# Two projection tiles in seven half-size block products, sums of weights on GpSimd, and rotary rows by transfers, in a two-layer hybrid decoder step

## What is computed

```python
h = rmsnorm(x, norm_g)
proj = h @ w_in                      # 1024 -> all columns below
qkv_a, z_a, beta, alpha, f_b, z_b, qkv_c, z_c, gate_raw = split(proj)
o_a = rmsnorm(gated_delta(silu(conv(qkv_a)), ...)) * silu(z_a)      # mixer a
o_b = rwkv7(token_shift_mix(f_b), ...)             * silu(z_b)      # mixer b
q_c = rope_partial(rmsnorm(q_c, qn_c), pos)                          # mixer c
k_c = rope_partial(rmsnorm(k_c, kn_c), pos)
o_c = attention(q_c, past_k + k_c, past_v + v_c)   * silu(z_c)
up    = [o_n @ w_branch[n] for n in (a, b, c)]       # 512 -> 1024
gates = sigmoid(gate_raw + b_gate)                   # 3 x 1024
x = x + sum(gates * up) @ w_out
x = x + sigmoid(x @ w_pg + b_pg) * (p @ w_ple)
```

## Time and profile before

| | us |
|---|---|
| median of 3 runs (1301.18 to 1306.65) | 1301.43 |
| profiled execution | 1299.52 |
| its span, first to last instruction | 1297.6 |
| PE busy, share | 1254.5, 97% |
| DVE busy, share | 594.6, 46% |
| ACT busy, share | 369.1, 28% |
| POOL busy, share | 136.8, 11% |
| mean granted TensorE clock | 0.993 |

### The profile page before, as it was taken

One profiled execution on the slowest core, in us unless ns is written; L12 is line 12 of the kernel. 1 busy time (PEld: TensorE's weight loads), 2 busy tenths in 40 slices (PEclk: granted clock), 3 DMA queues, 4 the chain that ended last, 5 costly groups with the idle time before them and its releaser, 6 DMA issues. The chain is left out here.

```text
span 1297.6 us, 23527 instructions
## 1 busy us (share of the span) xinstructions
PE 1254.5 (97%) x9334; PEld 954.2 (74%) x9334; DVE 594.6 (46%) x1269; ACT 369.1 (28%) x802; POOL 136.8 (11%) x204
## 2 busy tenths in 40 slices
PE   8999999999999999999999999999999999999998
PEld 6768866787687676767767787677866866767776
DVE  3655466644545523331254645475446454251212
ACT  2342212422233343310124322134124223433001
POOL 0112023020120110000001120210101101100000
PEclk9999999999999999999989999899999999999999
DMA  6832135412302565354245312543123035652631
GB/s 215 232 103 67 27 109 182 126 35 66 84 19 88 145 197 178 115 179 146 67 147 151 109 55 58 156 134 97 34 68 98 18 114 158 199 161 74 212 97 36
DMA packets 142215, 147.75 MB, mean 114 GB/s; under 512 B 15096, under 2 KB 129822, under 8 KB 141980
## 3 DMA queue, kind: packets, MB, share of 16 engines
q1 hardware_dynamic: 138492, 136.37, 34.5%
q0 software_dynamic: 3616, 9.89, 2.7%
HBM read 135.17 MB, written 11.07 MB: 113 GB/s over the span
## 5 line engine op out<-in xcount | busy, mean ns | idle before, releaser
L1073 PE MATMUL psum<-x_a,ring 128*128 128x288 f32 x1296 | 343.8, 416 | 2.3 <-ACT shift_in L1647 1.2
L1073 PE MATMUL psum<-x_b,ring 128*128 128x288 f32 x1296 | 338.5, 411 | 2.9 <-ACT shift_in L1647 1.2
L1073 PEld LDWEIGHTS psum<-x_a,ring 128*128 128x128 f32 x1296 | 242.2, 193 | 75.2 <-issue 13.8
L1073 PEld LDWEIGHTS psum<-x_b,ring 128*128 128x128 f32 x1296 | 239.0, 190 | 74.1 <-issue 15.0
L1647 ACT ACTIVATE arena<-psum 128x512 f32<-128x512 f32 (+9 forms) x206 | 96.8, 488 | 196.4 <-PE psum L1000 79.3
L1073 PE MATMUL psum<-z,ring 128*128 128x288 f32 x384 | 102.3, 413 | 1.2 <-issue 1.2
L1073 PEld LDWEIGHTS psum<-z,ring 128*128 128x128 f32 x384 | 70.1, 190 | 22.0 <-issue 4.8
L1000 PE MATMUL psum<-consts,arena 128*128 128x128 f32 (+2 forms) x446 | 64.2, 278 | 8.5 <-DMA arena<-in_x_prompt 5.5
L1000 PEld LDWEIGHTS psum<-consts,arena 128*128 128x128 f32 (+2 forms) x446 | 51.0, 144 | 27.3 <-issue 10.3
L1073 PE MATMUL psum<-merged,ring 128*128 128x288 f32 x256 | 62.6, 407 | 2.2 <-DVE merged L2099 2.2
L1647 ACT ACTIVATE arena<-arena 128x256 f32<-128x256 f32 (+7 forms) x104 | 44.8, 464 | 66.5 <-DVE arena L2577 27.9
(11 more groups left out here) (341 smaller groups left out, 1601.6 us busy)
## 6 DMA issues: line engine op xcount, KB each, us to landing
ring<-in_w_in SPq DMA_DIRECT2D x72, 1024.0 KB, 5.3
ring<-in_w_branch SPq DMA_DIRECT2D x24, 512.0 KB, 3.6
arena<-in_cache_k SPq DMA_DIRECT2D x32, 256.0 KB, 3.0
arena<-in_cache_v SPq DMA_DIRECT2D x32, 256.0 KB, 3.0
ring<-in_w_out SPq DMA_DIRECT2D x8, 1024.0 KB, 7.0
ring<-in_w_pg SPq DMA_DIRECT2D x8, 1024.0 KB, 4.9
arena<-in_state_dn SPq DMA_DIRECT2D x8, 512.0 KB, 8.3
out_dn_sample<-arena POOLq DMA_DIRECT2D x8, 512.0 KB, 4.7
```

What stands on the lines that cost most here:

```text
L1073: ins = mm(out[:, 0:NTOK], lhs, rhs(k), **flags)
```

## The change

**Pairs.** `p_z`, `p_c` and `p_g` are made two tiles at a time (`pair`, 24 pairs a layer). The 1024 x 256 block of weights and the 1024 x 288 block of h are each cut into 2 x 2 quarters: weights of 4 K-steps by 128 channels, h of 4 K-steps by 144 tokens. The 2 x 2 product is made in seven products of quarters instead of eight (the Winograd form). A pair is 14 "parts" of 2 K-steps, 4 instructions each, 56 instructions of 144 columns instead of 32 of 288, in two of the three banks. It needs

- four sums of h quarters per layer (`w_t`, VectorE, 128 x 576 each), written over X(l), which goes to DRAM (`x_kept`) in `a_conv(l,0)` and comes back in `p_g 23`, on SP's queue;
- four sums of weight quarters per pair (GpSimd, 128 x 512 each, 192 in all), after the parts 4, 8 and 12 of the pair before (`sums_at`); PE waits for them on `w_s` at parts 2, 4, 6 and 10;
- putting the products together: ScalarE copies one product (144 columns) after part 1 and two (288 columns) after part 5, VectorE does five additions of 144 columns after part 9, one after part 11 and one at the end. PE waits for ScalarE's copies (`w_kept`) at parts 6 and 10 and for VectorE's first two additions (`w_u`) at part 12. Before, ScalarE alone read these banks, and no later matmul of the same tile waited for that.

**Ring** of 3 places instead of 4. **Gates** leave PSUM without scale and bias; `g_tanh` is one operation of 288 columns per gate (8, 8, 6 and 2 of them) with scale and bias in it. **Rotary:** the permutation matmuls are gone. In `c_rms`, SP issues 6 transfers per tensor that move the rows to partner partitions (12 a layer), and 6 tiny ones turn the gains. VectorE does its three 1152-column operations in `c_rms`, ahead of the norm factor, and one in `c_rope`. **Order:** `FILL` is new, fillers are counted in parts, both `c_rms` stand together ahead of the cache fetches. Several semaphores are shared by steps that used one each.

```diff
-RING = 4
+RING = 3
+WIDE = ("p_z", "p_c", "p_g")
+PARTS = 14
...
+            def pair(l, part):
...
+                w, x, out = ((a11, b11, one[:, 0]), (WS[:, 0], t[:, 0], two[:, 0]), (a21, t[:, 2], two[:, 1]),
+                             (WS[:, 1], t[:, 1], one[:, 1]), (a12, b21, one[:, 2]), (WS[:, 2], b22, two[:, 2]),
+                             (a22, t[:, 3], one[:, 0]))[q]
...
+                elif part == 6:
+                    pe.wait_ge(S.sem("w_s"), 4 * no + 3)
+                    pe.wait_ge(S.sem("w_kept"), 2 * no + 1)
...
+                elif part == 12:
+                    pe.wait_ge(S.sem("w_u"), S.count("w_u"))
+                for k in (2 * (part % 2), 2 * (part % 2) + 1):
+                    ins = mm(out, w[:, k, :], x[:, k, :], start=k == 0, stop=k == 3, skip_group_check=True)
...
+                if m[-1] == 10:
+                    dve.wait_ge(S.sem("w_kept"), S.count("w_kept"))
+                    room_for(dve, order[final])
+                    tt(WP[:, 3, :], WP[:, 0, :], one[:, 1], ADD)
+                    tt(out[0], WP[:, 0, :], one[:, 2], ADD).then_inc(S.sem("w_u"), 1)
+                    dve.wait_ge(S.sem("w_u"), S.count("w_u"))
+                    link(tt(WP[:, 1, :], WP[:, 1, :], WP[:, 3, :], ADD))
+                    tt(out[3], WP[:, 1, :], WP[:, 2, :], ADD)
+                    link(tt(WP[:, 2, :], WP[:, 2, :], WP[:, 3, :], ADD))
...
+                    ins = (lambda: tt(WS[:, 0], a21, a22, ADD), lambda: tt(a21, a11, a21, SUB),
+                           lambda: tt(WS[:, 1], WS[:, 0], a11, SUB), lambda: tt(WS[:, 2], a12, WS[:, 1], SUB))[q]()
+                    ins.then_inc(S.sem("w_s"), 1)
...
-            def c_rope(l, i):
-                pe.wait_ge(S.sem("inv_roots"), S.count("inv_roots"))
-                pe.wait_ge(S.sem("c_rope"), S.count("c_rope", S.at - 1))
-                pe.wait_ge(S.sem("c_n"), S.count("c_n"))
-                for h in range(4):
-                    ins = mm(M[h][:, 0:NTOK], C("swap"), QC[:, 4 * i + h, :], start=True, stop=True)
-                ins.then_inc(S.sem("c_sw"), 1)
...
+                for to, of, n in turned:
+                    sp.dma_start(CSW[to:to + n, i, :, :], QC[of:of + n, 4 * i:4 * i + 4, :]).then_inc(S.sem(f"c_sw{i}"), 16)
...
-                fn(gates(n, part), gates(n, part), ACT.Tanh).then_inc(S.sem("g_tanh"), 1)
-                act.wait_ge(S.sem("g_tanh"), S.count("g_tanh"))
+                first, last = ((0, 7), (8, 15), (16, 21), (22, 23))[n + part]
+                evicted(act, "p_g", l, last)
+                for m in range(first, last + 1):
+                    ins = fn(gate(m), gate(m), ACT.Tanh, scale=0.5, bias=Phalf("b_gate", m))
```

More of the change, by code:

```diff
@@ L265 @@
     "c_qx": {"c_nat": (1, lambda st: st[2] == 0)},
+    "w_p": {"lead": (1, lambda st: st[2] in WIDE and st[-1] % 2 == 0)},
+    "w_kept": {"lead": (1, lambda st: st[2] in WIDE and st[-1] in (2, 6))},
+    "w_u": {"w_t": (1, None), "lead": (1, lambda st: st[2] in WIDE and st[-1] == 10)},
+    "x_moved": {"a_conv": (16, lambda st: st[2] == 0), "p_g": (16, lambda st: st[2] == 23)},
     "merged": {"p_up": (1, lambda st: st[2] > 0)},
@@ L268, with banks_of, sums_at @@
 }
+wide_lead = lambda st, part: st[0] == "lead" and st[2] in WIDE and st[-1] == part
 PROJECTIONS = ("p_a", "p_z", "p_ba", "p_f", "p_c", "p_g", "p_up", "p_y", "p_pg", "p_ple")
+def banks_of(st):
+    return 0 if st[0] not in PROJECTIONS else 2 if st[0] in WIDE else 1
+def sums_at(order):
+    ends = [i for i, st in enumerate(order) if banks_of(st)]
+    at, no = {}, 0
+    for before, last, i in zip([-1] + ends, ends, ends[1:]):
+        if order[i][0] not in WIDE:
+            continue
+        if order[last][0] in WIDE:
+            for part, qs in ((4, (0, 1)), (8, (2,)), (12, (3,))):
+                j = [j for j in range(before + 1, last) if wide_lead(order[j], part)]
+                at[j[0]] = [(no, q) for q in qs]
+        else:
+            j = [j for j in range(before + 1, last) if order[j][0] == "lead"]
+            at[j[0]] = [(no, q) for q in range(4)]
+        no += 1
+    return at
 class Steps:
@@ L279, in __init__ @@
             self.tally(name, [self.by(st, where) for st in order])
-        projections = [int(st[0] in PROJECTIONS) for st in order]
-        number = np.cumsum(projections) - 1
+        takes = [banks_of(st) for st in order]
+        first = np.cumsum(takes) - takes
         for b in range(3):
-            self.tally(f"bank{b}_read", [int(p and n % 3 == b) for p, n in zip(projections, number)])
+            self.tally(f"bank{b}_read", [sum((n + i) % 3 == b for i in range(k)) for k, n in zip(takes, first)])
+        sums = sums_at(order)
+        self.tally("w_s", [len(sums.get(i, ())) for i in range(len(order))])
     @staticmethod
@@ L480, in whole, with pair, branch_z @@
         out.append(s)
+    def pair(*s):
+        for a in range(PARTS - 1):
+            out.append(("lead",) + s + (a, a + 1))
+        out.append(s)
+    def branch_z(n):
+        for half in range(2):
+            pair("p_z", n, 2 * half + 1)
+            out.append(("z_silu", n, half))
     for m in range(NA):
@@ L2012, in y_out @@
                 fn(STG[96:128, 2, m // 4, :], y_banks(m)[2][96:128], ACT.Copy).then_inc(S.sem("y_rows_a"), 1)
-            do = dict(params_load=params_load, x_in=x_in, p_ple=p_ple, y_out=y_out, params=params, norm=norm, p_a=p_a, p_f=p_f, p_c=p_c, p_z=p_z, z_silu=z_silu, p_g=p_g, g_tanh=g_tanh, p_pg=p_pg, p_ba=p_ba,
+            do = dict(params_load=params_load, x_in=x_in, p_ple=p_ple, y_out=y_out, params=params, norm=norm, p_a=p_a, p_f=p_f, lead=lead, z_silu=z_silu, g_tanh=g_tanh, p_pg=p_pg, p_ba=p_ba,
                       a_convout=a_convout, a_silu=a_silu, a_sq=a_sq, a_beta=a_beta, a_l2=a_l2, a_rows=a_rows, a_scale=a_scale, a_pairs=a_pairs,
```

337 lines of the change are left out of this document (214 added, 123 removed), and 16 rows, old and new, of the table FILL.

## The result

The changed kernel takes **1456.23 us** (median of 4 runs, 1446.71 to 1459.3) against 1301.66 before on the same chip: 1.1165 times as long, 95% interval 1.1107 to 1.1224. I had forecast slower, 1317, with a range up to 1340. The direction was right; of 155 us I had foreseen 15. Some executions fall in a slower state of the chip, with a lower clock (here one of e9), and the ratios with an interval leave those out.

The account below looks back on a forecast made before the run. PE's nearly full matmul stream (97% busy) was taken as the bound. Per layer −25.2 (stream) + 12.5 + 16.0 (waits) + 4.4 (port) = +7.7, so +15.4 on 1299.5, 1314.9; as a median 1317 us, range 1283 to 1340.

Parts of the forecast that it names:

- The stream: PE's matmuls: 144-column instructions take 123 ns each; with the permutation matmuls gone, 25.2 us a layer saved, 50.4 in all.
- The order waits: PE waiting for ScalarE and VectorE, which work in order: 12.5 plus 16.0 us a layer lost.
- the 7.1 worked out: At b_lora(0,0), behind b_mix on VectorE: PE waits 7.1 us instead of 1.8.
- 5.14 for 4.1: At part 12 of p_c 5: PE waits 4.1 us for VectorE additions standing behind b_kk.
- 3.9 for 2.9: At the second c_rms, now right behind the first: PE waits 2.6 + 0.3 us for Ln and Exp.
- The term of 7.9 us a layer: Five pairs, p_c 9 to p_g 5, beside mixer b's chunk chain: three quarters of 10.5 us of VectorE additions delay PE.
- The 16.0 us a layer of that paragraph: Rest of the layer: waits of 7.9 beside the chunk chain, 3.3 at c_rms, 2.8 at gates, about 2.0 at softmax.
- The port: GpSimd's sums slow VectorE's SBUF operations: 2.9 us in b_mix and 1.5 in b_kk, 4.4 a layer (0 to 9.6).
- a bound of 9.6 us a layer: Port cost in b_mix and b_kk if each 4.8 us of GpSimd sums blocks VectorE whole, instead of 4.4.
- rival D: Clock falls behind PE's long waits add 7 to 14 us; with the port's cost whole, up to 1340; chance 0.25.
- Transfers: The 12 row transfers a layer on SP, ahead of the cache fetches: hidden by the stream of p_g, no cost.
- my sum without it gave 1308: Rival case: the sums of waits hold but the port costs nothing, 1317 − 9 = 1308; chance 0.15.

Follow-up runs that it names:

- e9: Changed kernel with GpSimd's sums cut to 8 columns for the 12 p_c pairs only, a quarter of all pairs: 1.0888 of before (1.074 to 1.1036).
- e1: Changed kernel with the same 192 GpSimd sums in the same places and with the same waits, but 8 columns each instead of 512: 1345.33 us.
- e11: Kernel of e1 with VectorE's seven additions per pair cut to 8 columns as well, waits kept: 1346.8 us.
- e12: Changed kernel with each pair's three VectorE additions of two SBUF inputs replaced by scaled copies of one input: 1437.23 us.
- e13: Kernel before with five GpSimd fills of 128 x 512 behind each of 96 tiles, reading nothing: 1308.07 us against 1300.63.
- e3: Kernel before with 192 GpSimd sums of 128 x 512 added, two behind each of 96 tiles, results unused: 1371.28 us.
- e5: Changed kernel with useless matmuls ahead of PE's waits, 80 at b_lora(l,0) and 30 at the second c_rms: 1456.61 us.
- e6: Kernel of e1 with useless matmuls ahead of PE's waits, 62 at b_lora(l,0) and 30 at the second c_rms: 1349.22 us.
- e15: Kernel before with the same six holds as e14, but PE does 62 useless matmuls in each: 1369.52 us.
- e10: Kernel before with the rotary part alone: row transfers and VectorE's new order in place of the permutation matmuls: 1295.81 us against 1300.06.
- e8: Changed kernel with 7 of the 12 parts ahead of both c_rms moved between them, in both layers: 1467.51 us.
- e14: Kernel before with PE held idle six times at p_f 1, 3 and 5 of both layers, until GpSimd finishes 20 fills: 1367.91 us.

## Why the prediction was right in sign and wrong in size

| | before | e1 | changed |
|---|---|---|---|
| time, us | 1301.66 | 1345.33 | 1456.23 |
| span | 1297.6 | 1342.7 | 1453.6 |
| PE busy | 1254.5 | 1237.7 | 1280.5 |
| span less PE busy | 43.1 | 105.0 | 173.1 |
| VectorE busy | 594.6 | 692.1 | 803.6 |
| mean granted clock | 0.993 | 0.969 | 0.939 |

**The stream.** In undisturbed stretches eight 144-column instructions start 0.98 us apart (216.07 to 217.05 in e1), 122.5 ns each. I had taken 123. Right.

```profile
216.07 1.14 PE L1208 MATMUL psum<-x_a,weight_sums 128*128 128x144 f32 x8
217.05 1.14 PE L1208 MATMUL psum<-x_a,ring 128*128 128x144 f32 x8
```

**The order waits.** I had summed 28.5 us a layer, 57 in all. e1, where GpSimd is out of the way, has 105.0 − 43.1 = 62 us more of idle PE. `b_lora` waits 7.08 us for the 7.1 worked out (up to 9.6 in the changed kernel). At `p_c 5` it is 5.14 for 4.1, at part 10 behind ScalarE and not at part 12 behind VectorE: the producer that is late (`b_kk`) is the same, the engine through which it reaches PE another. The second `c_rms` waits 3.9 for 2.9. The term of 7.9 us a layer, for additions of 2.1 us a pair in VectorE's queue, has no support: with 1.2 us a pair (e11) nothing changes. The 16.0 us a layer of that paragraph were otherwise not tested one by one. So that the sum of 57 lies near 62 is in part luck.

**The port: the step that failed.** I had read the stretching from the earlier trace rows, and priced it in two stretches a layer only, `b_mix` and `b_kk`: 4.4 us a layer, at most 9.6. It costs 111 us, 55 a layer, over ten times as much. Three things were missing in that step. First, the sums stand beside the whole middle of each layer: of the 819 VectorE operations without a PSUM input, 149 took over 0.1 us more than the shortest of their line and form, against 56 in e1. Second, an operation of 0.3 us can wait for a whole GpSimd operation of 1.3 us, so it loses by the number of meetings, not by its own length. The 93 further ones lost 112 us together, 1.2 us each, and a sum lasts 1.27; 0.6 us per us of overlap was the wrong measure. Third, PE waits for VectorE at many places in the chunk chains with little to spare, so the stretching passes through. From e1 to the changed kernel PE has 68 us more of idle time (173.1 − 105.0) and 43 us more of busy time (1280.5 − 1237.7), the latter with the lower clock. That their sum is just what VectorE lost is in part chance. The Trainium skill, "SBUF — State Buffer", section "Who interferes with whom", calls the loser fully blocked; by the rows above (0.3 us of work ending behind GpSimd's operations after 2.33, 1.36 and 2.01 us) the trace agrees. It names VectorE operations with two SBUF inputs, against a GpSimd operation that reads SBUF and not one that only writes, and those in a two-port mode, which it says a `tensor_scalar` can enter. Here one-input copies within SBUF, which are `tensor_scalar`, were stretched up to 2.29 us (e12), and fills on GpSimd cost 7 us against 70 (e13, e3), which agrees too. I had weighed this rule as a bound of 9.6 us a layer, again for two stretches only.

**The clock: a term that was missing.** The sum had nothing for it; only rival D had, 7 to 14 us. The mean fell to 0.939. PE's busy time should have been 1254.5 − 50.4 = 1204; it is 34 us above that in e1 and 76 in the changed kernel. The share of the clock that wasn't granted, times the span, grew by about as much over the 9 us of before, by 33 and 80 us. By that account the lower clock goes with up to 34 of e1's surplus of 44 and 43 of the port's 111. But it is an account, not a test: in e5 and e6 busying PE in its waits didn't shorten the kernel, and e15 took away too little to tell.

One thing on record speaks for a cost of its own. The kernel before ran 34 times beside the experiments, always the same program. The five executions with a mean clock of 0.997 or more took 1294.17 us in the median, the eleven with 0.991 or less 1304.43. They go together; which is the cause, they don't show. What part of the 76 us would remain if the clock alone were held is open.

**Transfers.** I had costed the twelve row transfers at nothing. That holds in the kernel before (e10 isn't slower), and in the changed kernel VectorE waited 0.19 us for them. It holds by the order alone: in e8 the same transfers held VectorE for 7.69 us, with additions queued behind that PE needed. I had looked at who waits for the transfers, and not at what is queued behind the waiting operation.

The chain, then: some 50 us less work for PE; 62 us more of idle time by order and 34 of busy time with the lower clock, so 44 us slower without the conflict of the sums, where my sum without it gave 1308; then 111 by the port, with the clock's share in it.

## What to carry to other kernels

Before giving "idle" GpSimd work on SBUF, ask for each VectorE operation beside it whether it reads PSUM: one that doesn't may wait for whole GpSimd operations that read SBUF, so the price goes by the number of meetings over the whole stretch, and a single stretched row in the old profile is a reason to price them all. To test it costs one run: add the GpSimd work with its results unused to the old kernel. And a faster stream is worth nothing across a place where its next piece needs an engine that is busy with something long; there the time saved comes back as waiting.

## What the hardware showed that was not expected

- 192 unused GpSimd sums of 128 x 512 (1.27 us each in the median) slowed a kernel by 70 us in which GpSimd was 11% busy; fills that kept it as busy cost 7 us.
- A VectorE copy from SBUF to SBUF with one input (0.235 us) was stretched up to 2.285 us beside such sums (e12). Of the 794 operations with a PSUM input in the changed kernel none was; L2226 took 303 to 305 ns in 48 cases.
- The 34 stretched additions of the pairs all ended 0.16 to 0.18 us behind a GpSimd operation; in the mean one such meeting cost 1.2 us.
- The stretched time is in the operation's duration and in no list of waits.
- Behind waits the stream of TensorE ran at 1.2 GHz for part of the time (e14: granted clock 0.50 over the first 4 us, 22 instructions of 288 columns in 8.65 us against 7.07), yet filling the waits with matmuls gave no gain in the whole that could be measured.
